# Even attention: the weighted sum of the two probability maps moved from one fused VectorE instruction to a VectorE scaling and a GpSimd addition

## The reference

```python
def diff_attend(q, k, v, lam):
    s = jnp.einsum('bqhmd,bkhmd->bhmqk', q, k).astype(jnp.float32) * (A_QK ** -0.5)
    p = jax.nn.softmax(s, axis=-1)
    a = p[:, :, 0] - lam * p[:, :, 1]
    return jnp.einsum('bhqk,bkhd->bqhd', a, v.astype(jnp.float32))

    # in even_mixer: 512 queries see 256 context and 512 own keys, 256 context queries the context alone
    o = lax.map(lambda qb: diff_attend(qb, k_all, v_all, lam), q_blocks)
    oc = diff_attend(qc.reshape(B, L, A_HEADS, 2, A_QK), kc, vc, lam)
```

## Time and profile before

| | |
|---|---|
| median of 3 runs | 2212.36 us (2211.63 to 2213.64) |
| profiled execution, its own time | 2212.97 us |
| its span | 2211.2 us |
| PE busy | 2139.8 us, 97% of the span |
| DVE busy | 1437.2 us, 65% |
| ACT busy | 555.2 us, 25% |
| POOL busy | 48.5 us, 2% |
| even attention | about 319 to 465 us of the span |

### The profile page before, as it was taken

How to read it: one execution, slowest core, us unless ns; L and a number is a source line. 1 busy time by engine, 2 the same in 40 slices (tenths; PEclk the granted TensorE clock), 3 DMA queues, 4 the chain that set the end, 5 groups by cost and what they waited for, 6 DMA issues and landing times.

```text
span 2211.2 us, 28161 instructions
## 1 busy us (share of the span) xinstructions
PE 2139.8 (97%) x11742; PEld 1761.6 (80%) x11742; DVE 1437.2 (65%) x1903; ACT 555.2 (25%) x1092; POOL 48.5 (2%) x31
## 2 busy tenths in 40 slices
PE   7999988899999999999999999999999999999998
PEld 4888875578788668878888888888888888888887
DVE  5797649885641665785887753654888437977633
ACT  3200028833222552382311110211100003111101
POOL 0000000000010110300000000000000000000000
PEclk8999999999899999999999999999999999999999
DMA  6544123222131112212222223222222222222322
GB/s 260 203 152 152 58 62 87 63 77 76 58 106 58 58 38 77 77 39 78 79 98 102 97 79 104 91 95 96 95 77 76 90 101 95 96 95 96 105 95 77
DMA packets 34416, 205.57 MB, mean 93 GB/s; under 512 B 4849, under 2 KB 5105, under 8 KB 14705
## 3 DMA queue, kind: packets, MB, share of 16 engines
q1 hardware_dynamic: 32912, 199.04, 26.2%
q10 hardware_dynamic: 1376, 4.72, 0.6%
HBM read 192.21 MB, written 2.10 MB: 88 GB/s over the span
## 4 chain that ended last, share of the span: by engine, by line
PE 86%; DVE 8%; ACT 3%; issue 2%; DMA 1%; DVEq 0%; SPq 0%; ACTq 0%
PE ps L458 23%; PE ps L459 23%; PE ps L460 22%; PE ps L557 3%; PE ps L558 3%; PE ps L559 3%; PE ps L712 2%; DVE stat L2259 1%; PE ps L1339 1%; PE ps L606 1%; PE ps L799 1%; ACT prob L1568 1%; PE ps L1031 1%; DVE h2lo L2062 1%; ACT h2hi L1380 1%
## 5 line engine op out<-in xcount | busy, mean ns | idle before, releaser
L458 PE MATMUL ps<-h2hi,whi 128*128 128x512 f32 (+1 forms) x1084 | 417.0, 385 | 3.4 <-DVE h2lo L2062 3.0
L460 PE MATMUL ps<-h2hi,wlo 128*128 128x512 f32 (+1 forms) x1084 | 412.6, 381 | 0.0
L459 PE MATMUL ps<-h2lo,whi 128*128 128x512 f32 (+1 forms) x1084 | 412.5, 381 | 0.0
L1940 DVE CAST whi<-raw 128x2048 fp32r<-128x2048 f32 (+2 forms) x148 | 172.2, 1164 | 344.8 <-DMA raw<-in_ffn_out 105.9
L1943 DVE TENSOR_TENSOR wlo<-raw,whi 128x2048 fp32r<-128x2048 f32 (+2 forms) x148 | 320.2, 2164 | 5.1
L458 PE MATMUL ps<-h1hi,whi 128*128 128x512 f32 (+1 forms) x768 | 269.7, 351 | 3.6 <-DVE h1lo L2144 1.4
L459 PE MATMUL ps<-h1lo,whi 128*128 128x512 f32 (+1 forms) x768 | 268.6, 350 | 0.0
L460 PE MATMUL ps<-h1hi,wlo 128*128 128x512 f32 (+1 forms) x768 | 266.5, 347 | 0.0
L458 PEld LDWEIGHTS ps<-h2hi,whi 128*128 128x128 f32 x1084 | 203.7, 188 | 44.8 <-DVE h2lo L2062 3.0
L460 PEld LDWEIGHTS ps<-h2hi,wlo 128*128 128x128 f32 x1084 | 203.7, 188 | 39.1
L459 PEld LDWEIGHTS ps<-h2lo,whi 128*128 128x128 f32 x1084 | 203.8, 188 | 37.9
(11 more groups left out here) (331 smaller groups left out, 3363.9 us busy)
## 6 DMA issues: line engine op xcount, KB each, us to landing
raw<-in_ffn_in SPq DMA_DIRECT2D x44, 1024.0 KB, 4.9
raw<-in_even SPq DMA_DIRECT2D x16, 1024.0 KB, 5.1
raw<-in_odd SPq DMA_DIRECT2D x12, 1024.0 KB, 4.9
raw<-in_sgu_v SPq DMA_DIRECT2D x12, 1024.0 KB, 4.9
raw<-in_sgu_u SPq DMA_DIRECT2D x12, 1024.0 KB, 5.0
raw<-in_sgu_out SPq DMA_DIRECT2D x16, 768.0 KB, 4.2
raw<-in_ffn_out SPq DMA_DIRECT2D x16, 704.0 KB, 4.0
raw<-in_ffn_out SPq DMA_DIRECT2D x11, 1024.0 KB, 4.9
```

The lines of the kernel that those rows point to most:

```text
L458: pe.matmul(o, r(lhi), r(rhi), start=first, stop=False, **kw)
L459: pe.matmul(o, r(lhi), r(rlo), start=False, stop=False, **kw)
L460: return pe.matmul(o, r(llo), r(rhi), start=False, stop=last, **kw)
L1940: step(dve.tensor_copy(whi[:, slot, 0:width].bitcast(F32R), raw[:, slot, 0:width]))
```

## The change

In each unit VectorE now only scales map 1 in place, `p[:, 1] *= weight` (a `tensor_scalar`), and signals a new semaphore `even_scaled`. GpSimd waits for it, adds the two maps into map 0, and signals `even_probs`, on which PE's transposes wait. The 48 additions stand in front of everything else in GpSimd's queue.

```diff
@@ -2283,8 +2283,8 @@
                 step(dve.scalar_tensor_tensor(out=stat[:, 16 + i:17 + i], in0=stat[:, 32 + u:33 + u], scalar=lam4[:, 3:4],
                                               in1=stat[:, 12 + i:13 + i], op0=ALU.mult, op1=ALU.mult))
                 p = prob[u % 3]
-                dve.scalar_tensor_tensor(out=p[:, 0, 0:n], in0=p[:, 1, 0:n], scalar=stat[:, 16 + i:17 + i],
-                                         in1=p[:, 0, 0:n], op0=ALU.mult, op1=ALU.add).then_inc(ea["probs"], 1)
+                dve.tensor_scalar(p[:, 1, 0:n], p[:, 1, 0:n], stat[:, 16 + i:17 + i], None, ALU.mult)\
+                    .then_inc(ea["scaled"], 1)
                 if u + 2 < len(EVEN_UNITS):
                     even_max(u + 2)
@@ -2686,6 +2686,12 @@
         @block.gpsimd
         def _(pool):
+            for u, (_, t, _) in enumerate(EVEN_UNITS):
+                n = TA if t < 4 else TC
+                p = prob[u % 3]
+                pool.wait_ge(ea["scaled"], u + 1)
+                pool.tensor_tensor(p[:, 0, 0:n], p[:, 0, 0:n], p[:, 1, 0:n], ALU.add).then_inc(ea["probs"], 1)
+
             pool.wait_ge(late_in, 32)
```

More of the change, by code:

```diff
@@ L298, in build_kernel @@
                                             "stack", "bank_shared", "copied", "pv", "out", "hi", "lo", "sq", "sums", "var", "root",
-                                            "inverse", "spread", "normed", "mixed", "lam", "lam_exp")}
+                                            "inverse", "spread", "normed", "mixed", "lam", "lam_exp", "scaled")}
         oa = {k: sem(f"odd_{k}") for k in ("scores", "negmax", "exp", "transposed", "bank_shared",
```

## The result

The changed kernel takes 2231.55 us (median of 4 runs, 2224.24 to 2232.28) against 2211.99 (4 runs, 2207.59 to 2213.64): 1.0085 of the time before, interval 1.007 to 1.010. In a second series it took 2227.59 us (6 runs), 1.0074 [1.0062, 1.0086]. The profiled execution took 2232.28 us with a span of 2230.5, 19.3 more than the one of before.

The account below looks back on a forecast made before the run. VectorE's 3.05 us per large unit was taken as the bound, with PE, VectorE and ScalarE nearly full. Terms 3.1 + 5.6 + 3.0 + 1.0 = 12.7 us gave 2225 us, 0.57% slower, range 2217 to 2237.

Parts of the forecast that it names:

- a ring: Engines awaiting each other in even attention: two-unit path grows from 4.89 to 6.35 us, 3.18 for one.
- (a): Large units in the middle of a pair: 0.13 us more for each, 3.1 us in all.
- (b): Last large unit of each pair: longer path exposed, 1.4 us four times, 5.6 us.
- (e): Small units otherwise: GpSimd's 0.73 us addition fits in, no cost.
- (c): Unit after the low parts in the first three pairs: path exposed, 1.0 us three times, 3.0 us.
- (d): End of the attention: last map later, partly covered; 1.0 us together with the unit before it.
- rival C: PE's clock falls more often in the attention's pairs: plus 6 to 10 us, 2231 to 2235 us; 20%.
- A: GpSimd's addition is quick and VectorE's relief shows in the large units: faster, about 2209 us; 5%.
- B: No measurable change: delay in the attention smaller or given back, about 2215 us, under 4.4 us; 12%.
- D: GpSimd hand-overs and its exclusion with VectorE in the attention cost more: 2230 to 2234 us; 13%.

Follow-up runs that it names:

- gaps_after: Changed kernel plus filler transposes on PE only in its longest waits; 2226.04 us, 1.0069 of the kernel before.
- after_again: The changed kernel itself, unaltered, run again as reference in a second series; 2227.59 us, 1.0074 of the kernel before.
- gaps_before: Kernel before plus filler transposes on PE only in its longest waits; 2212.83 us, 1.0007 of the kernel before.
- experiment 12: Against the kernel before, VectorE scales and then adds the maps in two instructions, GpSimd does nothing; 2229.12 us, 1.0075.
- relief_only: Changed kernel without the addition of the two maps (result incomplete), VectorE signals PE after scaling; 2207.02 us, 0.9986 of the kernel before.
- port_only: Changed kernel with maps not added; GpSimd makes equal-sized additions on other data, not awaited in the attention; 2207.73 us, 0.9988 of the kernel before.
- experiment 7: Kernel before with the two low-part subtractions of each pair moved from VectorE to GpSimd; 2213.41 us, 1.0011 of the kernel before.
- split_late: Kernel before, but the last 256 of each large unit's 768 columns are scaled by VectorE and added by GpSimd; 2209.51 us, 0.9992.
- filled_after: Changed kernel plus filler transposes on PE in its waits in all large units; 2222.2 us, 1.0056 of the kernel before.

## Why the prediction came out as it did

The direction was right, and so was the mechanism, a longer path round a ring. The sum of 12.7 us was a third below the measured 17.7 to 19.6, though; single terms of it were off both ways, and one was missing. Two readings tell where the rest lies.

**Pieces of the stage.** The pieces of (a), (b) and (e) are taken at a granted clock of 1.00 in both kernels; the changed kernel's fourth-pair 10.07 is that of gaps_after, as its own took 11.01 us at 0.85. Units 0 to 2 of the first three pairs are below 1.00 in both of these profiles: 9.16 us in the changed kernel at 0.51, 0.63 and 0.66 alike, and before 7.8 to 8.2 us at 0.81 to 0.85. In two other profiles one pair has them at full clock:

```profile
407.38:415.49 8.11, 6.21 (x50) 3.79 (x46) 7.07 (x11) 7.50 (x17) 3.63 (x2) 1.00 0.01 2
...
322.49:330.33 7.84, 5.39 (x41) 3.56 (x38) 7.70 (x11) 7.80 (x17) 0.00 (x0) 1.00 0.00 0
```

The first is the third pair of after_again (the changed kernel), the second the first pair of gaps_before. So most of the 1.1 us that these units took longer go with the clock, and the path has some 0.3 of it; one pair of each kernel is thin ground for that.

```
piece, changed minus before (us)                           measured    forecast
(a) units 3 to 7, four pairs: 12.9 - 11.45                 4 x 1.4     3.1
(b)+(e) 7 to 11, three pairs: 12.56 - 11.40 and the like   3 x 1.2     )
        fourth pair: 10.07 - 8.53                          1.5         ) 5.6
(c) unit 0 to 3, three pairs: 9.16 + 2.65 - 8.03 - 3.04    3 x 0.7     3.0
    the same, full clock: 8.11 + 2.65 - 7.84 - 3.04        3 x -0.1
    fourth pair: 9.27 - 9.14 (gaps_before)                 0.1
    last small to next pair, three times: 2.4 - 2.5        -0.3
(d) last scaling to first projection: 3.33 - 2.41          0.9         1.0
sum, with (c) as profiled                                  13.5        12.7
sum, with (c) at full clock                                11.1
```

- (a) The ring's new pace was forecast at 3.18 us and measured at 3.19 (2.79 and 3.59 us in turn; 3.22 over the four units). The old one, 3.05, holds for three of the four intervals only; the one into the last large unit, where VectorE reduces the maximum of a small unit (0.69 us) and not of a large one (1.76), was 2.31 us. The changed kernel took 2.81 there, and 3.68, 2.79 and 3.59 in the three before it. The forecast counted that interval as gaining 0.13 like the others. The term was 2.5 us too small.
- (b) and (e) 1.2 us a pair, 1.5 in the fourth, where 1.4 was forecast for the last large unit and nothing for the small ones: right in the main. The time shows in two intervals, from unit 7 to 8 (2.56 against 1.98) and from 8 to 9 (3.15 against 2.43 in the first pair). In the first VectorE's product of unit 8 is held by GpSimd until 352.11 (0.66 us), but nobody waits for that map. The second is the path: unit 9's exponentials stand behind the early copy of unit 7, for which ScalarE waited 1.63 us. From unit 9 to 11 the two kernels differ by only 0.1 us.
- (c) was too large. 1.1 us more at the low parts, at most, and 0.4 given back in the next unit, where VectorE is the bound (2.65 against 3.04), which I had not counted. At full clock next to nothing remains.
- (d) as forecast, and for the reason given: the addition of 256 took 0.97 us beside VectorE's cast, not 0.73.
- So the nearness of 12.7 to 11 or 13.5 is in part luck: (a) was 2.5 us too small and (c) 1 to 3 too large.
- The addition: 1.81 and 0.73 us, forecast 1.82 and 0.73 from the line through two other sizes. The scaling: 0.62, forecast 0.58. Hand-overs: 0.08 to GpSimd, 0.05 back. The factor 1.96 between GpSimd and VectorE that the Trainium skill states (GPSIMD Engine Reference, section 3.1) would have given 2.0 from the fused 1.02, an estimate; the trace stands at 1.81. Against VectorE's plain addition, 0.96 us in experiment 12, the ratio is 1.89.

**Runs at equal clock.** Each run has a mean granted clock beside its time. Over the 75 runs of the kernel before in the three series the mean is 2210.7 us at 0.9836, and a straight line through them rises by 1.2 us for each 0.001 less; it accounts for somewhat over half of their variance. The 10 runs of the changed kernel have a mean of 2228.6 us at 0.9801. By that line 4.2 us of their 17.9 go with the lower clock, and 13.7 remain at equal clock (12.6 to 14.8 by the scatter of the ten). A direct pair: at 0.981 eleven runs of before average 2214.0 us, two of the changed kernel took 2227.17 and 2228.01. But the line's price need not be the attention's. The mean is over the whole kernel, and the profiles show that a part of it is lost ahead of the attention (see relief_only); and the kernels of before with filling lie 4 to 5 us above the line. The two filled kernels, both at 0.986, are 9 us apart, though the one of before pays for filling that it has no room for. So 13.7 stands beside the 11 to 13.5 us of the pieces, and I take 11 to 14 us for the path.

The rest, some 4 to 7 us over the runs and 6 to 9 in the profiled execution (pieces (a) alone: 15.22, 15.36 and 14.37 against 12.87), goes with TensorE's clock: rival C, which I had kept out of the sum with a chance of 20% and a price of 6 to 10. The step that failed is there: the sum held no term for the clock, while in the stage whose PE share fell the mean granted clock fell from 0.94 to 0.86 (windows over the 137.36 and the 156.05 us). That the lower clock costs time in the attention is shown by the same pieces at both levels, within one kernel. That the longer waits are what brings it down is argued only: the one attempt that raised it in the attention (gaps_after, 0.91) came out 5 to 9 us shorter there in its profile, but as times neither filling was faster by more than its interval, and neither made the kernel before faster. The split between path and clock is known to a few us, not better.

**The rivals.** A (faster by the relief) fell on the addition's 1.81 us, and relief_only shows that even a free addition gives 3 to 4 us. B fell too: the loss is far above its 4.4 us, though the exposed places of (c) may have been nearly covered, as B had it. D: the hand-overs were as short as the base case had them, and the exclusion held a product here and there (351.45, 0.66 us), 247 ns on average against 220, 1.3 us of VectorE in the whole stage. At 351.45 nobody waited for it, and port_only shows that such holds cost the time nothing that can be measured. The Trainium skill's rule (SBUF — State Buffer, "SBUF: two separate sides": an exclusive lock for the whole instruction) and the rows of experiment 7 agree, but the changed kernel mostly runs its additions beside VectorE's maximum, which reads PSUM and takes its 1.76 us all the same.

## What to carry to other kernels

Before work is moved off a nearly full engine, ask what waits for its result: 0.4 us of relief for each unit was bought with 1.5 us on a path that others waited for, while the same offload of columns that are needed a unit later (split_late) cost nothing. A steady pace is read as a mean over several intervals, not from one. And where PE's share of a stage falls, price the clock as a term of the sum, from windows of the same work at either level. Last, before a gain is read from one profiled execution, look at where in the span it lies: 8.7 of relief_only's 10.4 us and all of filled_after's 5.8 lay outside the stretch from the first to the last combined map.

## What the runs showed of the hardware

- A VectorE product of two one-column tensors issued during a GpSimd operation is held until that ends: 1.72 us in place of 0.22, the price of the other's size and not its own. Maxima from PSUM ran beside additions at their usual 1.76 us, and so did the one-column reciprocal (0.16 us at 415.29 in port_only, inside the addition from 414.62).
- The clock differs between executions of the same kernel: 0.980 to 0.989 over the 75 runs of before, some 1.2 us for each 0.001, which goes with over half of the variance of those runs (2205.8 to 2216.65 us). Part of it is lost in the first 100 us, whose program is the same in all runs: their mean clock was 0.90 in the profile of before and 1.00 in that of relief_only, and the attention began at 325.17 and 316.43 us.
- The lower clock cost time where PE or the ring bounded (units 3 to 7 of the changed kernel: 12.87 us at 1.00, 14.37 at 0.88, 15.36 at 0.81) and none where VectorE did (unfused_vector: 13.50 to 13.55 us at 0.83 to 1.00).
- The fused scalar-tensor-tensor operation of 768 float32 elements took 1.02 us, the plain addition 0.96: the multiplication cost 0.06 us.
